# Summing a product over partitions in a modulation: one fp32 product against two fp32r products with split parts

## The reference, cut to what matters

```
c_act = silu(c_2)                                  # (1, 1024)
mod = c_act @ w_ada_2[0] + b_ada_2[0]              # (1, 3072)
shift, scale, gate = split(mod, 3)
h = rmsnorm(h_res, norm_w_2[0]) * (1 + scale) + shift
y = hybrid_mixer(h, ...)
h_res = h_res + gate * y
```

## Time and profile before

| | |
|---|---|
| median of 3 runs | 1887.53 us (1887.09 to 1888.59) |
| the profiled execution | 1887.14 us |
| its span, first to last instruction | 1885.3 us |
| PE busy | 1861.1 us, 99% of the span |
| DVE, ACT, POOL busy | 52%, 33%, 29% |
| the modulation's work lies in | 123 to 416 us |

### The profile page before, as it was taken

How to read it: one execution, slowest core, us unless ns; L and a number is a source line. 1 busy time by engine, 2 the same in 40 slices (tenths; PEclk the granted TensorE clock), 3 DMA queues, 4 the chain that set the end, 5 groups by cost and what they waited for, 6 DMA issues and landing times.

```text
span 1885.3 us, 26587 instructions
## 1 busy us (share of the span) xinstructions
PE 1861.1 (99%) x9993; PEld 1536.4 (81%) x9993; DVE 982.8 (52%) x2103; ACT 616.2 (33%) x1303; POOL 555.9 (29%) x927
## 2 busy tenths in 40 slices
PE   7999999999999999999999999999999999999998
PEld 7888888888888888888888787888887777788886
DVE  6646465774666433114777322223213777776665
ACT  6421111233444432101222202221114667655552
POOL 2112232232642221110101000222314777544442
PEclk9999999999999999999999999999999999999999
DMA  5314232356897845312221124665563776867663
GB/s 184 107 62 122 73 119 81 114 169 235 304 267 243 259 163 161 106 51 84 73 79 68 50 62 118 205 214 174 166 221 103 242 232 225 272 218 241 230 229 112
DMA packets 236364, 303.54 MB, mean 161 GB/s; under 512 B 41414, under 2 KB 161126, under 8 KB 236204
## 3 DMA queue, kind: packets, MB, share of 16 engines
q1 hardware_dynamic: 205724, 215.84, 36.9%
q0 software_dynamic: 23600, 77.61, 11.4%
q10 hardware_dynamic: 6912, 8.39, 1.2%
HBM read 194.71 MB, written 107.54 MB: 160 GB/s over the span
## 4 chain that ended last, share of the span: by engine, by line
PE 97%; DVE 1%; DMA 1%; issue 1%; ACT 0%; POOL 0%; SPq 0%; POOLq 0%; DVEq 0%
PE banks L145 26%; PE banks L147 26%; PE banks L146 26%; PE banks L2084 3%; PE banks L2047 3%; PE banks L2066 3%; PE banks L2682 2%; PE banks L2684 1%; PE banks L2375 1%; PE banks L1087 1%; PE banks L2067 1%; PE banks L2652 1%; PE banks L234 1%; DMA iraw<-in_w_in 0%; PE banks L1719 0%
## 5 line engine op out<-in xcount | busy, mean ns | idle before, releaser
L145 PE MATMUL banks<-hT,wu 128*128 128x512 f32 (+1 forms) x528 | 205.5, 389 | 2.2 <-DVE hT L220 2.2
L147 PE MATMUL banks<-hT,wu 128*128 128x512 f32 (+1 forms) x528 | 203.1, 385 | 0.0
L146 PE MATMUL banks<-hT,wu 128*128 128x512 f32 (+1 forms) x528 | 202.9, 384 | 0.0
L145 PE MATMUL banks<-iT,wub 128*128 128x512 f32 x384 | 151.3, 394 | 0.0
L145 PE MATMUL banks<-iT,wua 128*128 128x512 f32 x384 | 150.8, 393 | 0.0
L145 PE MATMUL banks<-wub,iT 128*128 128x512 f32 x384 | 150.6, 392 | 0.0
L147 PE MATMUL banks<-iT,wub 128*128 128x512 f32 x384 | 149.7, 390 | 0.0
L147 PE MATMUL banks<-iT,wua 128*128 128x512 f32 x384 | 149.5, 389 | 0.0
L146 PE MATMUL banks<-wub,iT 128*128 128x512 f32 x384 | 149.5, 389 | 0.0
L147 PE MATMUL banks<-wub,iT 128*128 128x512 f32 x384 | 149.5, 389 | 0.0
L146 PE MATMUL banks<-iT,wua 128*128 128x512 f32 x384 | 149.5, 389 | 0.0
(11 more groups left out here) (289 smaller groups left out, 4104.3 us busy)
## 6 DMA issues: line engine op xcount, KB each, us to landing
iraw<-in_w_in SPq DMA_DIRECT2D x36, 512.0 KB, 4.4
wa<-in_w_ada SPq DMA_DIRECT2D x48, 256.0 KB
yT<-sg POOLq DMA_DIRECT2D x32, 256.0 KB, 3.1
oraw<-yT SPq DMA_DIRECT2D x32, 256.0 KB, 4.6
xr<-in_x SPq DMA_DIRECT2D x16, 512.0 KB, 4.5
h<-h POOLq DMA_DIRECT2D x16, 512.0 KB, 4.1
hT<-tr POOLq DMA_DIRECT2D x16, 512.0 KB, 5.0
tws<-wg SPq DMA_DIRECT2D x16, 512.0 KB, 5.4
```

The costliest lines, as they stand in the source:

```text
L145: e.matmul(ps, lh, rh, start=first, stop=False)
L146: e.matmul(ps, lh, rl, start=False, stop=False)
L147: return e.matmul(ps, ll, rh, start=False, stop=last)
```

## The change

The sum over partitions is no longer one fp32 matmul. `acc` is split like the other operands: at step n = 18 + 8j ACT copies it, rounded to fp32r, into the `wa` tile that DVE has read last (`wah`, the same memory as `wa` under another type); at n = 19 + 8j DVE subtracts this from `acc` in place (`accl`, the same memory as `acc`); and at n = 20 + 8j PE makes two fp32r matmuls with the column of ones, one with the high and one with the low part, into the same bank. The semaphore `acc_step` counts ten steps in a block in place of eight. Since the high part stays in a `wa` tile until PE has read it, the load of x = 0 of the next block, which waited for DVE's eighth step, waits for PE's sum. `ones` becomes fp32r and is made by a memset and a copy at the start.

```diff
-        self.c, self.ones = k.at("c", 197.09375, [P, KT]), k.at("ones", 197.125, [P, 2])
+        self.c, self.ones = k.at("c", 197.09375, [P, KT]), k.at("ones", 197.125, [P, 2], F32R)
+        self.accl, self.wah = k.at("accl", 198, [P, W], F32R), [k.at(f"wah{i}", 200 + 2 * i, [P, W], F32R) for i in range(2)]
+    def acc_high(self, j):
+        return self.wah[(9 * j + 7) % 2][:]
...
# SP, ada(i)
-                if (i - 2) % 9 < 8:
-                    w.wait_ge(*self.acc_step.ge((i - 2) // 9 * 8 + (i - 2) % 9 + 1))
+                if (i - 2) % 9 == 7:
+                    w.wait_ge(*self.summed.ge((i - 2) // 9 + 1))
+                elif (i - 2) % 9 < 7:
+                    w.wait_ge(*self.acc_step.ge((i - 2) // 9 * 10 + (i - 2) % 9 + 1))
...
# ACT, step n, after its other work and before out.ahead_act
+            if n + 2 in self.sum_at:
+                j = self.sum_at[n + 2]
+                w.wait_ge(*self.acc_step.ge(10 * j + 8))
+                e.activation(self.acc_high(j), self.acc[:], ACT.Copy).then_inc(*self.acc_step.inc())
...
# DVE, at its start
-        e.memset(self.ones[:], 1.0).then_inc(*self.const_v.inc())
+        e.memset(self.acc[:, 0:2], 1.0).then_inc(*self.const_v.inc())
+        w.wait_ge(*self.const_v.last())
+        e.tensor_copy(self.ones[:], self.acc[:, 0:2]).then_inc(*self.const_v.inc())
...
# DVE, step n, before the gate and out.ahead_dve
+            if n + 1 in self.sum_at:
+                j = self.sum_at[n + 1]
+                w.wait_ge(*self.acc_step.ge(10 * j + 9))
+                e.tensor_tensor(self.accl[:], self.acc[:], self.acc_high(j).bitcast(F32), ALU.subtract).then_inc(*self.acc_step.inc())
...
# PE, step n in sum_at
-                w.wait_ge(*self.acc_step.ge(8 * j + 8))
-                w.wait_ge(*self.const_v.ge(1))
+                w.wait_ge(*self.const_v.ge(2))
+                w.wait_ge(*self.acc_step.ge(10 * j + 10))
...
-                e.matmul(self.pa[0:1, :], self.ones[:, 0:1], self.acc[:], start=True, stop=True).then_inc(*self.summed.inc())
+                e.matmul(self.pa[0:1, :], self.ones[:, 0:1], self.acc_high(j), start=True, stop=False)
+                e.matmul(self.pa[0:1, :], self.ones[:, 0:1], self.accl[:], start=False, stop=True).then_inc(*self.summed.inc())
```

More of the change, by code:

```diff
@@ L529, in ada @@
             elif x < 8:
-                w.wait_ge(*self.acc_step.last())
+                w.wait_ge(*self.acc_step.ge(10 * j + x))
                 e.scalar_tensor_tensor(out=acc[:], in0=wa[:], scalar=self.c[:, x:x + 1], in1=acc[:],
```

## The result

| | before | change |
|---|---|---|
| median of 10 runs | 1888.02 us (1886.55 to 1889.0) | 1892.8 us (1890.63 to 1894.77) |
| ratio to before | | 1.0021, 95% interval 1.0013 to 1.0029 |
| span of the profiled execution | 1885.3 us | 1890.5 us |
| start of the next stage (first L145 on ws and ys) | 416.87 us | 420.84 us |

The change is slower, by 0.21% or 4 to 5 us; the forecast was 1887.4, which is 0.1 us under the 1887.53 that it started from, with a range up to 1891.3. PE's new products are as cheap as forecast, and the new wait at the sixth sum is there. It is longer than forecast, TensorE's clock falls as it ends, and there is a second new wait that the prediction did not have.

What follows compares the result with a forecast made beforehand. PE's matmul stream was taken to bound the kernel; five sums gaining 3.5 us against the sixth's 0.7 saved and 3.9 to 4.1 waited gave -0.1 us, so 1887.4 us, range 1883.3 to 1891.3.

Steps and rivals of the forecast that it cites:

- the sum: PE up to n = 61: five sums gain 3.5 us, the sixth saves 0.7 and waits 3.9 to 4.1: -0.1 us.
- PE bounds, and a sum costs 1.17 us against 0.47: PE's stream, busy 99%: each sum saves 0.70 us, six fully hidden 4.2 us.
- Operands of blocks 0 to 4 in time: First five sums: no PE wait; tightest is block 4, with 2.8 us to spare.
- The sixth operand is late, behind the splits and the gate of n = 58: Block 5, DVE's n = 59: operand ready at 403.3, PE waits 3.9 us on the clock of before.
- DVE's chain comes 5 x 0.70 = 3.5 us earlier with PE: Block 5: DVE's chain starts at PE's end of n = 53, so its 403.3 comes 3.5 us earlier.
- After that PE had no wait: After the sixth sum: no PE wait until later stages, whose small waits move with it; nothing added.
- The clock rival: After the sixth sum's wait: PE's clock falls to half pace, costing up to 2.0 us, 1889.4; chance 0.13.
- The fixed chain: Block 5: DVE's chain does not move with PE, the wait becomes 7.4 us, 1890.9; chance 0.12.
- costly products: PE's sums: one-column fp32r products save nothing, block 5 still waits 3.9 us, 1891.5; chance 0.06.

Runs made afterwards that it cites:

- products alone: Kernel before with two fp32r products per sum reading a rounded acc, no copy, subtraction or new wait: 1884.18 us, ratio 0.9982.
- the run with the split first: The change with block 5's copy on ACT before n = 58's evacuation and its subtraction on DVE before n = 58's gate and splits: 1888.32 us.
- the sum put later: The change with the sixth sum one step later on PE (n = 61) and its bias at n = 62: 1884.59 us, ratio 0.9983.
- wait alone: The change's copy, subtraction and PE wait, but each sum stays one plain fp32 product of acc: 1896.48 us, ratio 1.0047.
- unit-first run: The change with DVE's low part of the second gate unit made before the two steps of acc at n = 16, 32, 48: 1891.63 us.
- the control: Kernel before with plain fp32 sums, sixth sum one step later and second gate unit's low part before the acc steps: 1888.73 us, ratio 1.0.

## Why the prediction was wrong, point by point

The forecast had -0.1 us against before, and the median came out 4.8 us above. In the trace, up to the next stage, it was +4.0 us. Three terms make the difference: the sixth wait was 1.3 us longer than forecast, and two terms that the sum put at nothing measured 1.4 us (a weight's low part at n = 35) and 1.6 us (the clock).

- *PE bounds, and a sum costs 1.17 us against 0.47.* Right. The products alone gained some 4 us where 4.2 was said.
- *Operands of blocks 0 to 4 in time.* Right; no sum but the sixth waits.
- *The sixth operand is late, behind the splits and the gate of n = 58.* Right in place and cause, shown by the run with the split first and by the sum put later. **The wait was mis-sized**: 5.2 us where 3.9 was forecast. Of the 1.3 us too little, 0.6 are the subtraction's length: the step took 0.65 us from a quiet row, while the row at that very place showed 1.25.
- *DVE's chain comes 5 x 0.70 = 3.5 us earlier with PE.* **This step failed in its size.** It does move with PE, but PE at n = 53 was only 2.1 us earlier (evacuation at 359.36 against 361.49), for it had waited at n = 35; and of those 2.1 us 1.5 were left at n = 59: block 4's store was still 2.1 us earlier (364.59 against 366.72), but the two tables behind it took 9.26 us where they had taken 8.90, and the rest went before DVE's n = 56. PE itself was 2.1 us earlier at the sixth sum, so 0.6 us more of waiting came of it.
- *After that PE had no wait.* The prediction looked for late operands of the sums and for nothing else. It looked neither at what PE, once earlier, would find missing nor at what DVE's extra work would delay. **The low part of `wu` at n = 35 was not costed**: 1.4 us. The trace of before had it, in these rows of DVE's and PE's timelines:

```profile
244.74 1.57 DVE L498 TENSOR_TENSOR wu<-rawg,wu 128x1024 fp32r<-128x1024 f32 x1
```

```profile
246.74 0.39 PE L145 MATMUL banks<-hT,wu 128*128 128x512 f32 x1
```

  The low part ended at 246.31 and PE began n = 35 at 246.74: 0.43 us to spare. Two cheaper sums would take 1.4 if DVE stayed; with the products alone DVE came along, and nothing waited. What PE waited for was a load that came later: block 1's store landed 2.9 us after its issue, not 1.6, and the loads behind it, DVE's steps and the low part followed. The wait alone shows that this is enough: PE was not earlier there, the store took 2.6 us, and PE waited 0.5.
- *The clock rival* was priced near, 2.0 us at most against 1.6 measured, but 2.0 and 2.6 in two other runs, and given 0.13. **The sum put the clock at nothing**, and of the three terms it was the one most off. In the trace of before every wait of PE above 2 us lay at the start, and products did come at half pace behind it, though the profile's clock reads 1.00 there. The Trainium skill, TensorE: Matmul & The Clock Gate, Part 1, says that an idle array falls back to 1.2 GHz, and the trace after agrees, with 0.54 granted behind the wait of 5.0 us. With this term in the forecast and all else as it was, the time would have been 1889.4.
- *The fixed chain* and *costly products* fall, the first by the unit-first run, the second by the products alone.

What stays open. The load that DVE waited for at n = 32 came late because the store of block 1's result (`mod`) took 2.6 to 2.9 us to land in all eight runs that have the copies and subtractions, and 1.6 us before, with the products alone and in the control. The stores of blocks 0, 2, 3 and 4 took 1.6 us in all of them. The eight also have the moved wait on SP, so which part of the change does it is not shown. Other transfers are no likely reason: in the change the DMA engines stood at a share of 0.00 to 0.04 from 222 to 228 us. The difference of 1 to 4 us behind the modulation was not looked into either.

## What to carry to other kernels

An engine that is busy 99% of the time gains from a cheaper instruction only while every operand still beats it: when a change adds steps to an operand's chain, read on the producing engine which instructions stand before it at its new place, and take durations from the rows at that place. Then shift the busy engine by what it gains and look again at each close arrival, also those the change does not touch. A wait of some microseconds on TensorE is to be priced with the clock that falls behind it, and moving the consumer by one step of the loop can cost nothing and bring most of the gain, as the sixth sum put later did here.

## What the runs showed of the hardware that I had not expected

- An fp32r product with one column of weights costs what one of 128 columns costs, 0.23 us in the stream for 512 columns; a plain fp32 one costs 1.17 us, five times as much.
- After PE's wait of 5.0 us the clock stood at its lower level while PE was already busy again, until 406 us in the change and until about 407 and 410.7 in the unit-first run and the wait alone, with the same length of wait; it cost 1.6, 2.6 and 2.0 us. Waits of 0.9, 1.0 and 1.1 us left it at 1.00.
